# An RWKV chunk stage with chunks of 64 tokens on the quadrants of the array, and an output stage fused with the branch products

## What is computed

```python
def _rwkv7_scan(s0, w, k, v, kk, a, r=None):
    def step(s, xt):
        wt, kt, vt, kkt, at = xt[:5]
        sa = jnp.einsum('bhvk,bhk->bhv', s, -kkt)
        s = (s * wt[:, :, None, :] + sa[..., None] * (kkt * at)[:, :, None, :]
             + vt[..., None] * kt[:, :, None, :])
        return s, jnp.einsum('bhvk,bhk->bhv', s, xt[5])
...
def _branch_merge(ret_o, rwkv_o, st, qu, lp):
    y_ret = (jax.nn.silu(qu['ret_g']) * (_head_norm(ret_o, RET_EPS) * lp['ret_gn_g']).astype(dt)) @ lp['w_br_ret']
    bonus = jnp.sum(qu['r'][None] * st['k'] * r_k, axis=-1, keepdims=True).sum(0) * st['v']
    y_rw = (_head_norm(rwkv_o, RWKV_EPS) * lp['rwkv_ln_g'] + lp['rwkv_ln_b']).astype(dt)
    y_rw = ((y_rw + bonus.reshape(bonus.shape[:-2] + (-1,))) * qu['rwkv_g']) @ lp['w_br_rwkv']
    g_ret, g_rw = jnp.split(qu['merge'], 2, axis=-1)
    return (g_ret * y_ret + g_rw * y_rw) @ lp['w_out']
```

## Time and profile before

| | |
|---|---|
| median of 3 runs | 4440.33 us (4437.95 to 4442.67) |
| the profiled execution | 4433.51 us, its span 4431.7 us |
| mean granted TensorE clock | 0.960 of 2.4 GHz |
| busy, share of the span | PE 92%, DVE 56%, ACT 49%, POOL 14% |
| DMA | 681.68 MB, mean 154 GB/s |

### The profile page before, as it was taken

The page is one execution under the profiler, slowest core; times in us unless marked ns, Lnnn a source line. Parts: engine busy times, 40 slices in busy tenths (PEclk is TensorE's granted clock), DMA queues, the critical chain, the costliest instruction groups (busy, mean ns, idle before and its releaser), DMA issues. The chain is left out here.

```text
span 4431.7 us, 71788 instructions
## 1 busy us (share of the span) xinstructions
PE 4086.9 (92%) x28554; PEld 3415.2 (77%) x28554; DVE 2475.9 (56%) x3784; ACT 2154.5 (49%) x3251; POOL 616.9 (14%) x682
## 2 busy tenths in 40 slices
PE   7999999999899999999999696989679999999993
PEld 5878778888688888888888575868568888888883
DVE  5533425333277777777777686335544554544545
ACT  5434435333277777777677246114224444444443
POOL 1000000000222222222222033210000000000000
PEclk9999999999899999999999895999789999999997
DMA  6555555454522112211221438655436666566567
GB/s 242 194 191 179 181 183 157 152 160 149 155 61 65 55 55 57 70 55 55 57 63 33 133 94 263 207 195 171 187 134 227 201 217 216 202 226 203 214 218 275
DMA packets 345392, 681.68 MB, mean 154 GB/s; under 512 B 33228, under 2 KB 237108, under 8 KB 326552
## 3 DMA queue, kind: packets, MB, share of 16 engines
q1 hardware_dynamic: 323000, 591.39, 39.8%
q0 software_dynamic: 22112, 86.41, 6.5%
HBM read 530.10 MB, written 147.60 MB: 153 GB/s over the span
## 5 line engine op out<-in xcount | busy, mean ns | idle before, releaser
L112 PE MATMUL fro__acc<-fro__hT_hi,fro__wh 128*128 128x512 f32 (+1 forms) x1608 | 626.1, 389 | 7.5 <-DVE fro__hT_lo L2514 4.6
L113 PE MATMUL fro__acc<-fro__hT_hi,fro__wl 128*128 128x512 f32 (+1 forms) x1608 | 613.6, 382 | 0.0
L114 PE MATMUL fro__acc<-fro__hT_lo,fro__wh 128*128 128x512 f32 (+1 forms) x1608 | 613.4, 381 | 0.0
L2520 DVE TENSOR_TENSOR fro__wl<-prj__w,fro__wh 128x1024 fp32r<-128x1024 f32 x201 | 246.1, 1225 | 640.1 <-ACT fro__wh L2324 640.1
L1998 DVE TENSOR_TENSOR pre__wl<-fin__raw,pre__wh 128x4096 fp32r<-128x4096 f32 x96 | 424.7, 4424 | 316.2 <-ACT pre__wh L1948 316.2
L1948 ACT ACTIVATE pre__wh<-fin__raw 128x4096 fp32r<-128x4096 f32 x96 | 348.6, 3631 | 192.6 <-PE exp__acc L114 192.5
L112 PE MATMUL exp__acc<-pre__wh,exp__xh 128*128 128x512 f32 x1024 | 401.3, 392 | 0.7 <-DVE exp__xl L2003 0.7
L114 PE MATMUL exp__acc<-pre__wl,exp__xh 128*128 128x512 f32 x1024 | 398.8, 389 | 0.0
L113 PE MATMUL exp__acc<-pre__wh,exp__xl 128*128 128x512 f32 x1024 | 398.7, 389 | 0.0
L112 PEld LDWEIGHTS fro__acc<-fro__hT_hi,fro__wh 128*128 128x128 f32 x1608 | 304.4, 189 | 73.8 <-issue 18.2
L113 PEld LDWEIGHTS fro__acc<-fro__hT_hi,fro__wl 128*128 128x128 f32 x1608 | 304.6, 189 | 59.0 <-issue 3.6
(11 more groups left out here) (452 smaller groups left out, 8322.6 us busy)
## 6 DMA issues: line engine op xcount, KB each, us to landing
fin__raw<-in_w_x SPq DMA_DIRECT2D x96, 2048.0 KB, 7.9
prj__w<-in_w_z SPq DMA_DIRECT2D x201, 512.0 KB, 3.9
s_zT<-fro__zo SPq DMA_DIRECT2D x128, 256.0 KB, 4.3
fro__wm<-in_w_mod POOLq DMA_DIRECT2D x16, 1024.0 KB, 5.5
brp__gate<-s_zT SPq DMA_DIRECT2D x32, 512.0 KB, 4.9
s_y<-rwc__yo SPq DMA_DIRECT2D x37, 256.0 KB, 2.3
prj__xin<-in_tokens SPq DMA_DIRECT2D x18, 512.0 KB, 5.6
rwc__kS<-s_kS SPq DMA_DIRECT2D x36, 256.0 KB, 3.1
```

Source lines behind the costliest of these rows:

```text
L112: pe.matmul(out, sh, mh, start=first, stop=False)
L113: pe.matmul(out, sl, mh, start=False, stop=False)
L114: return pe.matmul(out, sh, ml, start=False, stop=last)
L2520: ve.tensor_tensor(wl[s % 3][:, :, :], w[s % 3][:, :, :], wh[s % 3][:, :, :], ALU.subtract).then_inc(split_lo, 1)
```

## The change

In the chunk stage the chunks become 64 tokens. A slab is 128 tokens of one direction, so there are 36 slabs as there were 36 halves. Its two chunks lie on partitions 0 to 63 and 64 to 127, and everything that is a matrix per chunk (masks, T, X, errors, refinements) is 64x64 on the quadrant of rows and columns that belongs to the chunk, both chunks in one PSUM bank. There are 5 levels. The steps that follow the state (`from_state`, `solve`, `state`, `outputs`) run twice for a slab, once for each chunk, in the order of the direction. The output is made with tokens on partitions and stored by token. Buffers `AR`, `BK` and the turned operands are threefold. The refinements are plain float32 with one rounded copy by DVE.

The two stages behind retention become one, `rwkv_mix`. Its lists go in steps `s` from -5; step `s` from 0 to 63 is one product of 12 matmuls. Tile `t` of the RWKV output starts at step `base(t)` and is spread over the steps behind it; its result stays on chip as half of the moving operand. y comes by token, so the turn of the sum goes. The branch products have 4 PSUM banks instead of 8, one gate per product, and single instead of double buffers for the split inputs. `ywT` is neither written nor read.

```diff
-    C = P
-    NG, GH = 2, 4
-    LEV = 6
+    C, HC, NG, GH, LEV, B = P, 64, 2, 4, 5, 3
...
-        AR = [sb(f"AR{d}", [P, 4, 2, C]) for d in range(2)]
+        AR = [sb(f"AR{u}", [P, 4, 2, C]) for u in range(B)]
-        BK = [sb(f"BK{d}", [P, WH, 4, C]) for d in range(2)]
+        BK = [sb(f"BK{u}", [P, WH, 4, HC]) for u in range(B)]
-        MB = (XB, PB, XB, TTP)
+        MB, RB = (XB, TP), (EB, PB[0])
...
-            def masked(q, d, at, ahead):
-                ve.wait_ge(S["m1"], at("m1", q + 1, ahead) + START)
-                for o in range(2):
-                    tt(BK[d][:, 2 * q + o, :, :], f4(MB[q][o]), quad[:, d, :, :], ALU.mult).then_inc(S["m1d"], 1)
+            def masked(j, z):
+                ve.wait_ge(S["m1"], at("m1", j, z + 1))
+                if j >= B:
+                    ve.wait_ge(S["ym"], at("ym", j - B))
+                for o in range(2):
+                    tt(BK[j % B][:, GH * z + o:GH * z + o + 3:2, :, :].rearrange("p q k c -> p q (k c)"),
+                       MB[z][o][:, :].rearrange("p (q m) -> p q m", q=2),
+                       quad[:, j % 2, :, :].rearrange("p k c -> p (k c)")[:, None, :].to_broadcast([P, 2, 4 * HC]), ALU.mult).then_inc(S["m1d"], 1)
...
-                    pe.wait_ge(S["tbc"], at("tbc", 2 * l + g + 1) + START)
-                    for h in range(GH):
-                        m = mm(f4(XB[g])[:, h, :], ATb[:, g, h, :], Tb[:, g, h, :], start=True, stop=True)
-                    m.then_inc(S["xm"], 1)
+                for g in range(NG):
+                    pe.wait_ge(S["tbc"], at("tbc", j, 2 * l + g + 1))
+                    for h in range(GH):
+                        for z in map(side, range(2)):
+                            m = mm(h4(XB[g])[z, h, :], ATb[z, g, h, :], Tb[z, g, h, :], start=True, stop=True)
+                    m.then_inc(S["xm"], 1)
...
-                    for h in range(GH):
-                        m = mm(f4(TP[g])[:, h, :], TTb[:, g, h, :], Xb[:, g, h, :], start=False, stop=l == LEV - 1, skip_group_check=True)
-                    m.then_inc(S["tm"], 1)
+                    for h in range(GH):
+                        for z in map(side, range(2)):
+                            m = mm(h4(TP[g])[z, h, :], TTb[z, g, h, :], Xb[z, g, h, :], start=False, stop=l == LEV - 1, skip_group_check=True)
+                    m.then_inc(S["tm"], 1)
...
+                    pe.wait_ge(S["yc"], at("yc", j - 1))
+                for n in range(WH):
+                    c = slice(WD * n, WD * n + WD)
+                    for t in range(2):
+                        z, o = side(turn_of(j, t)), side(1 - turn_of(j, t))
+                        mm(PB[t][z, c], BK[u][z, n, 2, :], v_t[u][z, c], start=(n == 0), stop=False, skip_group_check=True)
...
+                for q in range(4):
+                    c = slice(P * q, P * q + P)
+                    hb = Hb[j % 2][:, q, :, :].rearrange("p o c -> p (o c)")
+                    m = mm(PB[t][z, c], AR[u][:, q, 0, z], hb, start=False, stop=True, skip_group_check=True)
+                    m = mm(PB[t][o, c], AR[u][:, q, 1, z], hb, start=False, stop=False, skip_group_check=True)
+                m.then_inc(S["rhm"], 1)
...
+            def solve(j, t):
+                z = side(turn_of(j, t))
+                pe.wait_ge(S["rhc"], at("rhc", j, t + 1))
+                pe.wait_ge(S["gd"], at("gd", j))
+                if t:
+                    pe.wait_ge(S["hadd"], at("hadd", j, 1))
+                for n in range(WH):
+                    c = slice(WD * n, WD * n + WD)
+                    m = mm(EB[z, c], Gr[z, n // GH, n % GH, :], R[z, c], start=True, stop=True)
+                m.then_inc(S["uum"], 1)
...
+            def state(j, t):
+                u, z = j % B, side(turn_of(j, t))
+                pe.wait_ge(S["uc"], at("uc", j, t + 1))
+                for key, val in ((kappa_t[u], v_t[u]), (beta_t[u], U)):
+                    for n in range(WH):
+                        c = slice(WD * n, WD * n + WD)
+                        m = mm(EB[side(n % 2), WD * (n // 2):WD * (n // 2) + WD], key[z, c], val[z, c],
+                               start=(val is not U and n < 2), stop=val is U, skip_group_check=True)
+                m.then_inc(S["sm"], 1)
...
+            def outputs(j, t):
+                u, s = j % B, turn_of(j, t)
+                z, o = side(s), side(1 - s)
+                pe.wait_ge(S["uc"], at("uc", j, t + 1))
+                for n in range(WH):
+                    c = slice(WD * n, WD * n + WD)
+                    m = mm(PB[t][o, c], BK[u][z, n, 1, :], U[z, c], start=False, stop=True, skip_group_check=True)
+                m.then_inc(S["ym"], 1)
...
+            for h in range(SLABS):
+                p, n = h - 1, h + 1
+                more = n < SLABS
+                inverse_seed(h)
+                if h:
+                    refine(1, p, 0)
+                    refine(1, p, 1)
+                if more:
+                    learning(n)
+                couple(0, h)
+                if h:
+                    refine(2, p, 0)
+                    refine(2, p, 1)
+                double(0, h)
+                if h:
+                    values(p)
+                couple(1, h)
+                if h:
+                    from_state(p, 0)
+                double(1, h)
+                couple(2, h)
+                if h:
+                    solve(p, 0)
+                double(2, h)
+                if h:
+                    state(p, 0)
+                couple(3, h)
+                if h:
+                    outputs(p, 0)
+                double(3, h)
+                if h:
+                    from_state(p, 1)
+                couple(4, h)
+                if h:
+                    solve(p, 1)
+                double(4, h)
+                if more:
+                    pairs(n, 0)
+                    pairs(n, 1)
+                if h:
+                    if more:
+                        state(p, 1)
+                    outputs(p, 1)
+                if more:
+                    turn(n, 0)
+                errors(h, 0)
+                errors(h, 1)
+                if more:
+                    turn(n, 1)
+                    turn(n, 2)
+                refine(0, h, 0)
+                if h + 2 < SLABS:
+                    decays(h + 2)
+                refine(0, h, 1)
+                if more:
...
```

```diff
-def rwkv_output(nc, T):
...
-def branch_products(nc, T):
...
+def rwkv_mix(nc, T):
...
+    def base(t):
+
+        return 2 * t - 4 if t < 4 else 16 * (t // 4) - 12 + 4 * (t % 4)
+    tile_at = {base(t): t for t in range(NL)}
+    chunk_at = {-4: 0, -3: 1, -2: 2, -1: 3, 1: 4, 2: 5, 3: 6, 4: 7}
+    FIRST, LAST = -5, UNITS + 2
...
+            def both(t):
+                ve.wait_ge(y_in[t % B], 32 * (t // B + 1) + START)
+                yt = y[t % B]
+                ve.tensor_tensor(yt[:, 0, :], yt[:, 0, :], yt[:, 1, :], ALU.add).then_inc(ys_ok, 1)
...
+            def products(i):
+                n, j, m = unit(i)
+                if m == 0:
+                    pe.wait_ge(y_lo[j], n + 1 + START)
+                if i >= 4:
+                    pe.wait_ge(gated, i - 3 + START)
+                c = slice(m * P, (m + 1) * P)
+                for k in range(4):
+                    if n == 0 and m == 0:
+                        pe.wait_ge(w_lo, 4 * j + k + 1 + START)
+                    mm = product(pe, acc[i % 4][:, :], (wh[:, j, k, c], wl[:, j, k, c]), (yh[j][:, k, :], yl[j][:, k, :]), k == 0, k == 3)
+                mm.then_inc(made, 1)
+            for s in range(FIRST, UNITS):
+                if s - 1 in tile_at:
+                    spread_bonus(tile_at[s - 1])
+                if s - 3 in tile_at:
+                    turn_rows(tile_at[s - 3])
+                if s >= 0:
+                    products(s)
+
...
+            for s in range(FIRST, LAST):
+                if 0 <= s - 1 < UNITS:
+                    gates(s - 1)
+                if s in tile_at:
+                    stats(tile_at[s])
+                if s + 1 in tile_at:
+                    both(tile_at[s + 1])
+                if s - 1 in tile_at:
+                    scales(tile_at[s - 1])
+                if s - 2 in tile_at:
+                    bonus(tile_at[s - 2])
+                if s in chunk_at:
+                    j = chunk_at[s]
+                    ve.wait_ge(w_hi, j + 1 + START)
+                    ve.tensor_tensor(wl[:, j // 4, j % 4, :], stage[j % NS][:, :], wh[:, j // 4, j % 4, :], ALU.subtract).then_inc(w_lo, 1)
+                if s == -4:
+                    low(0, 0)
+                if s >= 0 and s % 16 == 11 and s // 16 + 1 < NB:
+                    low(0, s // 16 + 1)
...
+            for s in range(FIRST, LAST):
+                if s - 3 in tile_at:
+                    weighted(tile_at[s - 3])
+                if s in tile_at:
+                    root(tile_at[s])
+                if s - 1 in tile_at:
+                    normed(tile_at[s - 1])
+                if s in chunk_at:
```

(14 more changed lines are left out.)

1503 lines of the change are left out of this document (690 added, 813 removed).

## The result

The change takes 4372.68 us, the median of 4 runs (4363.24 to 4381.16), against 4439.26 (4 runs) before: ratio 0.985, interval 0.983 to 0.987. It is faster, by 67 us, and the forecast was 4276 us, a gain of 164. The time is inside the wide range (4150 to 4410) and outside the forecast's own (4235 to 4320); 60% of the gain did not come.

What follows compares the result with a forecast made beforehand. TensorE (PE) was taken as the bound. Gains of 123 us in the chunk stage and 41 from fusing output and branch products, 164 in all, gave 4276 us; own range 4235 to 4320, wide range 4150 to 4410.

Steps and rivals of the forecast that it cites:

- quadrants in turn: Chunk stage: diagonal quadrants writing one PSUM bank take turns, 58 ns instead of 29 per record; 4625 us, chance 0.11.
- 25.9 us of streaming: Chunk stage: sum of PE's matmul, transpose and other work per slab, 4.1 us less than for an old half.
- 3.1 + 2.1: Chunk stage, per slab: 3.1 us of PE waits on the serial chain plus 2.1 for fourteen array-shape switches.
- The term for `double(3)`: Chunk stage: PE waits 0.9 us because `levels(3)` is queued on DVE behind four `state` operations of 0.42 us.
- term for `state(p, 0)`: Chunk stage: PE waits 0.5 us because ACT's copy of U sits behind `scale_bk` and its 1.28 us table load.
- the small matmuls are faster still: Chunk stage: 64x64 bf16 matmuls spaced 14 ns rather than 29, perhaps 2.5 us less per slab; 4186 us, chance 0.17.
- the waits eat the gain: Chunk stage: slab stays at 34 us, 4378 us, chance 0.15; sign: PE waits for ACT's or DVE's copies above 5 us.
- the clock rival: Chunk stage: shorter matmuls with gaps let PE drop to 1.2 GHz, 12 us more per slab; 4700 us, chance 0.05.
- PE stays about 90% occupied: Chunk stage: the argument against a drop of PE to 1.2 GHz, a case given chance 0.05.
- the slab of 31.1 us as a mean: Chunk stage: PE streaming, waits and switches per 128-token slab, 3.2 us less than an old half's 34.3.
- 27.5 us for the tiles' work in the products: Fused stage: bonus spreads and transposes 21.5 us, their switches 4, and 2 of wait, added to 177.5 of products.
- beside the products: Fused stage: DVE, ACT and POOL work of the tiles overlaps the products; tiles add some 57 us to DVE's 66.

Runs made afterwards that it cites:

- weights_first_timed: The change plus quadrant fillers, later first state update and later row turning, with ScalarE's weight rounding reordered in the fused stage; 4241.1 us, ratio 0.956 to the kernel before.
- fill_all: The change plus 64 idle matmuls a slab, put before twelve steps where PE waits in the chunk stage; 4366.7 us.

## Why the prediction was partly right

**Right.** The direction, and about the sum at full clock: with the clock held, the chunk stage took 1149.1 us against 1148.4 forecast, and a slab 31.2 against 31.1. That they meet within 1 us is luck: there are 32 pairs of fillers in it, and two errors of the sum cancel (next paragraph). Both quadrants do work at once, so the rival of quadrants in turn falls. The lead-in of the fused stage was shorter than forecast by 5 us, its tail as forecast, and no wait of PE in the products is put down to a DMA (193 GB/s in the stage, 215 forecast).

**Right by two errors that cancel.** The 25.9 us of streaming were too high. In the slab of 31.30 us above, the steps of at most 0.135 us between starts of matmuls add to 19.0 us: the levels' 240 records cost 4.3 instead of 7.0, `values` 1.0 instead of 1.4, `pairs` 1.6 instead of 2.6. Conversely the larger steps, waits and changes of the array's shape, add to 12.2 us where the text had 3.1 + 2.1. The term for `double(3)` was 0.9; it was 2.2 a slab over ten slabs, since the state update took 3.2 us and not 1.7. The term for `state(p, 0)` was 0.5 and is 1.1. The rival "the small matmuls are faster still" was right about its 14 ns, and right that the waits would then show, but not how much. The waits for ACT and DVE are 5.6 us a slab, over the 5 that were the sign of "the waits eat the gain"; yet with the clock held and most of them still there a slab takes 31.2 and not 34, so they ate little by themselves.

**Wrong: the clock rival, priced as if it were separate.** The step that failed is "Against: PE stays about 90% occupied", chance 0.05, and with it the slab of 31.1 us as a mean. PE was busy 84% of the chunk stage, and even in the slab of 31.30 us 12.2 us, 39%, go into steps over 0.135 us. The granted clock was 0.83, stretches of up to 13.7 us per slab ran at 1.2 GHz, and the mean slab took 33.3. The size in the rival (12 us a slab) was off the other way: the fillers give back 2.1, and the clock's whole cost is near 4 by the estimate above, since part of what runs at half speed hides in the waits. Filling the waits gave 77 of the missing 97 us, shown by the timed runs. I read the 0.88 of retention as a hint and did not ask what the waits that I had just added up would do.

**Wrong: 27.5 us for the tiles' work in the products.** The products took 29 us more than forecast. Some 6 to 9 were the turn of the rows one step too early, 5 to 7 ScalarE's order of work at the start; both are waits on the engines that I had called "beside the products". The rest, some 14 us (218.7 in weights_first_timed against 205), is not settled.

## What to carry to other kernels

When a change makes TensorE's work smaller and its waits more numerous, count the waits first: one of 1.5 us per half cost another 1.3 through the clock here, and some 7 us of waits in a slab cost at least another 2.1. If such waits can't be removed, fill them with matmuls that nobody reads; it is worth the trial, since 32 pairs of them a slab took 77 us off, while twice as much filling (fill_all) gave most of the gain back. Where a wait is moved, give it work to stand behind in the same edit; moved alone, it came back whole. And fill only where TensorE's own work is on the path: at the start of the fused stage a higher clock gave nothing.
